# Differential attention of a hybrid layer: values stationary in column halves, heads in pairs, head norm in turned form

## What is computed

```python
lam = jnp.exp(jnp.sum(lp[0] * lp[1])) - jnp.exp(jnp.sum(lp[2] * lp[3])) + lam_init
...
logits = jnp.einsum('bqhrd,bshrd->bhrqs', qb, k).astype(jnp.float32) * (dq ** -0.5)
p = jax.nn.softmax(jnp.where(visible, logits, NEG_INF), axis=-1)
a = (p[:, :, 0] - lam * p[:, :, 1]).astype(v.dtype)
return jnp.einsum('bhqs,bshd->bqhd', a, v)
...
return head_rmsnorm(out, norm_g) * (1.0 - lam_init)
```

## Time and profile before

| | us |
|---|---|
| median of three runs (1865.95 to 1866.45) | 1865.99 |
| the profiled execution, whole | 1862.66 |
| its span | 1860.9 |
| TensorE, VectorE, ScalarE busy | 1735.6, 1454.9, 941.6 |
| D units, 397.4 to 670.3 | 272.9 |
| C and A pairs, 670.3 to 970.7 | 300.4 |

### The profile page before, as it was taken

How to read it: one execution, slowest core, us unless ns; L and a number is a source line. 1 busy time by engine, 2 the same in 40 slices (tenths; PEclk the granted TensorE clock), 3 DMA queues, 4 the chain that set the end, 5 groups by cost and what they waited for, 6 DMA issues and landing times. The chain is left out here.

```text
span 1860.9 us, 24050 instructions
## 1 busy us (share of the span) xinstructions
PE 1735.6 (93%) x8722; PEld 1313.2 (71%) x8722; DVE 1454.9 (78%) x2094; ACT 941.6 (51%) x1207; POOL 152.1 (8%) x129
## 2 busy tenths in 40 slices
PE   7999999999999999999999989759999999999980
PEld 7768877777777777777767767647777777777750
DVE  5587869989788878766529965669999999999966
ACT  6533121133334445545556610138877878777752
POOL 1100000000000000000000000012122122122103
PEclk9999999999999999999999999769999999999995
DMA  5202222112443322323216810379999999999937
GB/s 198 68 11 82 85 75 69 57 57 74 155 140 120 111 69 63 140 64 98 85 46 243 332 51 34 151 278 369 388 397 407 394 398 402 396 397 400 405 118 287
DMA packets 75920, 358.76 MB, mean 193 GB/s; under 512 B 8636, under 2 KB 11228, under 8 KB 49340
## 3 DMA queue, kind: packets, MB, share of 16 engines
q1 hardware_dynamic: 66364, 324.08, 46.8%
q0 software_dynamic: 5888, 20.97, 3.4%
q10 hardware_dynamic: 3584, 12.58, 1.7%
HBM read 301.63 MB, written 55.98 MB: 192 GB/s over the span
## 5 line engine op out<-in xcount | busy, mean ns | idle before, releaser
L2357 DVE TENSOR_TENSOR wa_lo<-wa,w_hi 128x2048 fp32r<-128x2048 f32 x127 | 287.5, 2286 | 14.9 <-ACT w_hi L2270 13.5
L2270 ACT ACTIVATE w_hi<-wa 128x2048 fp32r<-128x2048 f32 x127 | 242.8, 1915 | 63.0 <-PE psum L2215 36.4
L1470 PE MATMUL psum<-h_hi,w_hi 128*128 128x512 f32 x512 | 212.7, 415 | 4.2 <-DVE w_lo L153 2.1
L1470 PE MATMUL psum<-h_hi,w_lo 128*128 128x512 f32 x512 | 205.2, 401 | 0.0
L1470 PE MATMUL psum<-h_lo,w_hi 128*128 128x512 f32 x512 | 202.5, 395 | 0.0
L167 DVE MAX8 top<-sel 128x8 f32<-128x384 f32 (+5 forms) x192 | 171.4, 893 | 4.8
L2364 DVE TENSOR_TENSOR wb_lo<-wd,w_hi 128x2048 fp32r<-128x2048 f32 x64 | 143.8, 2289 | 33.9 <-ACT w_hi L2279 33.9
L165 DVE MATCH_REPLACE8 sel<-top,sel 128x384 f32<-128x384 f32 (+5 forms) x192 | 168.2, 876 | 0.0
L2199 PE MATMUL psum<-w_hi,xT_hi 128*96 128x512 f32 x512 | 164.5, 402 | 1.9 <-DVE xT_lo L2372 1.9
L2199 PE MATMUL psum<-w_hi,xT_lo 128*96 128x512 f32 x512 | 160.6, 394 | 0.0
L2199 PE MATMUL psum<-wa_lo,xT_hi 128*96 128x512 f32 x512 | 160.5, 395 | 0.0
(11 more groups left out here) (372 smaller groups left out, 3380.6 us busy)
## 6 DMA issues: line engine op xcount, KB each, us to landing
wa<-expert_up SPq DMA_DIRECT2D x128, 1024.0 KB, 10.4
wd<-expert_down SPq DMA_DIRECT2D x64, 1024.0 KB, 10.5
w<-w_gate SPq DMA_DIRECT2D x32, 512.0 KB, 4.2
gate_pre<-gate_out SPq DMA_DIRECT2D x64, 256.0 KB, 3.3
gate<-gate_pre SPq DMA_DIRECT2D x32, 512.0 KB, 5.7
ys<-yo ACTq DMA_DIRECT2D x32, 384.0 KB, 6.9
w<-w_T SPq DMA_DIRECT2D x18, 512.0 KB, 3.9
ys<-zeros SPq DMA_DIRECT2D x7, 1152.0 KB, 5.9
```

The lines of the kernel that those rows point to most:

```text
L1470: ins = nc.tensor.matmul(psum[:, 7, :], w[:, k, :], x[:, k, half * 512:(half + 1) * 512], start=(n == 0), stop=(n == BURST - 1))
L2270: nc.scalar.activation(hi_a(j, q).rearrange("p c m n -> p (c m n)"), wa[j][q][:, :, :, :].rearrange("p c m n -> p (c m n)"), ACT.Copy).the ...
L2357: nc.vector.tensor_tensor(wa_lo[j][q][:, :, :, :].rearrange("p c m n -> p (c m n)"), wa[j][q][:, :, :, :].rearrange("p c m n -> p (c m n)" ...
```

## The change

1. **Weights times values in D** as in C and A: values stationary, two heads together, after the turns of the second head; the first head of a pair has no `weigh`. All turns of a unit come at once. `weigh` is one function now.
2. **First map scaled by ScalarE.** `inverse` (VectorE) and `scale` (ScalarE) run for D too: `scale(u)` stands behind the second exponential and ahead of `gate_store`, `inverse(u)` behind `maxima(u)`. `differ` waits for `scaled`. `norm` only copies, one unit later for blocks 0 to 6.
3. **Head norm of D in turned form.** The output is already turned, so the 16 transposes go. Squares at NB + 2; then a string of 4 matmuls with a 128 x 128 matrix of two 64 x 64 blocks of ones, after unit NB + 8, sums them over each head's partitions (f32, 512 columns each); ScalarE takes the root of 512 columns each, four times; VectorE takes the reciprocal of the whole [128, 2048] in place at NB + 12 and multiplies at NB + 13. At NB + 3, NB + 8 and NB + 9 selections stand now.
4. B's string comes after unit 11 instead of 10. GpSimd sets the matrix of ones (3 memsets). The gain is loaded as [128, 2]. SyncE stores D at k = 41 from q2, behind `y_ready`.

```diff
-    s.gainB, s.gainD = sb("gainB", [P, W], 197.25), sb("gainD", [P, W], 198.25)
+    s.gainB, s.gainD = sb("gainB", [P, W], 197.25), sb("gainD", [P, 2], 198.25)
...
-    Y_AT = {"D": 10, "C": 16}
+    Y_AT = {"D": 11, "C": 8}
...
+                        if n == 0:
+                            sp.wait_ge(pt_copied, copied_by["B"])
+                        else:
+                            sp.wait_ge(y_ready, 2)
+                        sp.dma_start(s.yT_back[n], (s.k1, s.q2)[n][:, :, :]).then_inc(yT_stored, 16)
...
+            link(pool.memset(halves[:, :], 0.0))
+            link(pool.memset(halves[0:HD, 0:HD], 1.0))
+            pool.memset(halves[HD:P, HD:P], 1.0).then_inc(halves_ready, 1)
...
+                    if what == "D":
+                        act.wait_ge(aneg_ready, 1)
+                        nc.scalar.activation(sq[:, c, t0 * P:(t0 + 4) * P], src, ACT.Sqrt, bias=eps[:, 0:1],
+                                             scale=1.0 / HD).then_inc(pt_copied, 1)
...
                 if u < NB:
                     act.wait_ge(stats_ready, n_exp[u] + 2)
                     diff_exp(1)
+                    scale(u)
                 if u and u - 1 in burst_after:
                     gate_store(burst_after[u - 1])
...
-                link(nc.vector.reciprocal(inv[:, :], sums[:, b % 2, :, 0]))
-                nc.vector.tensor_tensor(token_heads(kind, b),
-                                        psum[:, 6, 0:W].rearrange("p (c h d) -> p c h d", c=2, d=HD),
-                                        by_head(inv[:, :]), ALU.mult).then_inc(out_normed, 1)
+                nc.vector.tensor_copy(out_of[kind][:, :, b * P:(b + 1) * P],
+                                      psum[:, 6, 0:2 * P].rearrange("p (c n) -> p c n", c=2)).then_inc(out_normed, 1)
...
-                link(nc.vector.scalar_tensor_tensor(out=stat[:, v % 4, 5:6], in0=stat[:, v % 4, 4:5],
-                                                    scalar=sums[:, b % 2, h, 0:1], in1=lam[:, 4:5],
-                                                    op0=ALU.mult, op1=ALU.mult))
+                link(nc.vector.tensor_tensor(stat[:, v % 4, 5:6], stat[:, v % 4, 4:5], lam[:, 4:5], ALU.mult))
+                dve.wait_ge(scaled, v + 1)
...
+                y, h = s.q2, u % NH
                 if u == NB + 2:
+                    nc.vector.tensor_tensor(sq[:, :, :], y[:, :, :], y[:, :, :], ALU.mult).then_inc(squared, 1)
+                elif u == NB + 12:
+                    dve.wait_ge(pt_copied, copied_by["D"])
+                    link(nc.vector.reciprocal(sq[:, :, :], sq[:, :, :]))
+                elif u == NB + 13:
+                    for c in range(2):
+                        ins = nc.vector.scalar_tensor_tensor(out=y[:, c, :], in0=y[:, c, :], scalar=gain_T[:, c:c + 1],
+                                                             in1=sq[:, c, :], op0=ALU.mult, op1=ALU.mult)
...
                 maxima(u)
+                inverse(u)
...
+                    if what == "D":
+                        pe.wait_ge(squared, 1)
+                        pe.wait_ge(halves_ready, 1)
+                        nc.tensor.matmul(psum[:, 4 + i % 2, :], halves[:, :], sq[:, c, t0 * P:(t0 + 4) * P],
+                                         start=True, stop=True).then_inc(pt_ready, 1)
...
+                for g in range(n):
+                    if i + g >= 2:
+                        pe.wait_ge(pt_copied, i + g - 1)
+                    turn(i + g)
+                for g in range(2):
+                    gate(gates_before(what) + (2 + g) * quarter, quarter)
+                    if h % 2 and g < n:
+                        m = weighed[0]
+                        weigh(i - n + g, i + g, m + g, m + n + g, 2 if n == 1 else 1 + 2 * g)
```

More of the change, by code:

```diff
@@ L991, in attend @@
     pt = [sb(f"pt{i}", [P, 512], 155.25 + 2 * i) for i in range(4)]
-    sq = sb("sq", [P, NT * NH, HD], 163.25)
+    sq = sb("sq", [P, 2, SEQ], 163.25)
+    halves = sb("halves", [P, P], 203.5)
     bias = sb("bias", [P, NH, BAND], 112.25)
@@ L1341, in inverse @@
                 _, b, h = units[u]
-                dve.wait_ge(exp_done, n_exp[u + 1])
+                dve.wait_ge(exp_done, n_exp[u] + 1)
                 nc.vector.reciprocal(stat[:, u % 4, 6:7], sums[:, b % 2, h, 0:1]).then_inc(inv_ready, 1)
             def more(u):
-                heads = q_of["D"][:, :, :].rearrange("p c (n d) -> p (c n) d", d=HD)
-                h = u % NH
+                y, h = s.q2, u % NH
                 if u == NB + 2:
[L1350 to L1362, removed]
+                    nc.vector.tensor_tensor(sq[:, :, :], y[:, :, :], y[:, :, :], ALU.mult).then_inc(squared, 1)
[6 more added lines that the diff above has]
+                                                             in1=sq[:, c, :], op0=ALU.mult, op1=ALU.mult)
+                    ins.then_inc(y_ready, 1)
                 else:
@@ L1430, in _, with weigh @@
             values = {"D": s.v2, "C": s.v1, "A": s.v2}
[L1432 to L1434 removed]
+            def weigh(i0, i1, m0, m1, freed):
+                u, g0, ng, last = groups[i0]
                 kind, b, h = units[u]
                 k0, nk = keys(kind, b)
[L1437 to L1458 removed]
+                pe.wait_ge(pt_copied, i1 + 1)
+                if h == 0 and g0 == 0 and u:
+                    pe.wait_ge(out_normed, u // NH)
+                for j in range(ng):
+                    for r, m in enumerate((m0, m1)):
+                        ins = nc.tensor.matmul(psum[HD * r:HD * r + HD, 6, h // 2 * P:(h // 2 + 1) * P],
+                                               values[kind][:, k0 + g0 + j, (h + r) * HD:(h + r + 1) * HD],
+                                               pt[m % 4][:, j * P:(j + 1) * P],
+                                               start=(g0 + j == 0), stop=(g0 + j == nk - 1))
+                ins.then_inc(pv_done, freed)
             def gate(first, count):
@@ L1482, in weigh_waiting @@
                     i = waiting.pop()
-                    weigh(i, weighed[0])
-                    weighed[0] += 1 if units[groups[i][0]][0] == "D" else 2
+                    weigh(i, i + 1, weighed[0], weighed[0] + 1, 2)
+                    weighed[0] += 2
             def turn(i):
@@ L1533, in _ @@
                     continue
-                if i >= 2:
-                    pe.wait_ge(pt_copied, i - 1)
-                quarter = BURST // 4
-                if g0 == 0:
-                    if what + 1 < NB:
-                        score(what + 1, 1)
-                    else:
-                        score(NB, 2)
-                    if what:
-                        gate(gates_before(what), 2 * quarter)
-                    pe.wait_ge(diff_ready, what + 1)
-                turn(i)
-                if last:
-                    gate(gates_before(what) + 2 * quarter, quarter)
-                weigh_waiting()
-                waiting.append(i)
-                if last:
-                    gate(gates_before(what) + 3 * quarter, quarter)
-                    weigh_waiting()
+                if g0:
+                    continue
+                quarter, n = BURST // 4, 1 if last else 2
+                if what + 1 < NB:
+                    score(what + 1, 1)
+                else:
+                    score(NB, 2)
+                if what:
+                    gate(gates_before(what), 2 * quarter)
+                pe.wait_ge(diff_ready, what + 1)
+                for g in range(n):
[7 more added lines that the diff above has]
+                        weigh(i - n + g, i + g, m + g, m + n + g, 2 if n == 1 else 1 + 2 * g)
+                if h % 2:
+                    weighed[0] += 2 * n
             weigh_waiting()
```

61 lines of the change are left out of this document (14 added, 47 removed).

## The result

| | us |
|---|---|
| median after (7 runs, 1871.8 to 1873.68) | 1873.10 |
| median before, run beside it (7 runs, the three shown before among them) | 1868.02 |
| ratio | 1.0032, interval 1.0023 to 1.0041 |
| profiled execution after, its span | 1873.68, 1871.9 |

The account below looks back on a forecast made before the run. TensorE, 93% busy, was taken as the bound. The terms -11.6 - 0.3 + 0.5 + 0.45 + 10.2 + 1.9 = +1.15 gave a median of 1867.1 us, no change that can be told; range 1861.5 to 1872.5 us.

Parts of the forecast that it names:

- Step 1: Weights times values in D with values stationary, two heads together: TensorE gains 11.6 us, from 31.0 to 19.4.
- The number of switches is the same 80: TensorE in D: switches between gates, weighing and scores stay at 80, so the change adds no switching cost.
- the upper of the two values given: Gain of weighing in D: 11.6 us taken, or 12.5 if 0.1 more ahead of scores in some last groups is counted.
- holds both: TensorE in D: C's 1.03 us for eight products already includes parallel tiles and the loss at each switch of mode.
- Step 2: First map of D scaled by ScalarE ahead of the gate store: costs nothing, with a cover that thins.
- 0.7 to 1 us: ScalarE's gate store in D's narrower blocks: slack left before TensorE needs bank 7, with the scaling ahead of it.
- Step 3: B's string, one unit later in D: +0.5 us, with the granted clock falling behind it again.
- it falls again, at the same price: Behind B's string the granted clock falls to 0.50 as before, at an unchanged cost.
- Step 4: D's string of four float32 products and roots: 2.85 us instead of 2.42, +0.45.
- Step 5: VectorE's 2048-column reciprocal in C: 12.1 us, stalling TensorE once by 10.2 us, plus 1.9 for the clock.
- rival B: VectorE at NB + 12: reciprocal of 14.7 us or more; at 17 us, stall 15.1 and time 1872.0 us; chance 0.12.
- The 0.3 that the border was to give back: Border from D to C: the changes around scaling and norm give back about 0.3 us, summed as -0.3.

Follow-up runs that it names:

- the second traces: The kernel before and the changed kernel, each run once more with no edit: 1866.2 us (ratio 0.9999) and 1872.93 us (ratio 1.0034).

## Why the prediction was wrong

**Step 1, where it failed.** `weigh` was worth 12.5 us (31.8 to 19.3), the upper of the two values given. The failed sentence is "The number of switches is the same 80", by which the gates around `weigh` cost nothing more. Leaving the turns aside, the traces have 128 changes of work in D before and 104 after; of these, changes of the tile's shape are 64 before and 104 after. The old `weigh` had the shape of the gates, and only the scores had another. Now the 24 groups of `weigh` have a third shape, 16 of them in the middle of the gates and 8 ahead of the scores, and in the 24 other places the gates end at the scores, where a `weigh` of their own shape stood between. Between the second traces the gates of the 32 units grow by 4.3 us (184.4 to 188.7), and the 48 ends of 0.09 us alone come to that. The prediction had set 0.9 us against such ends, which is why it took 11.6 and not 12.5; the term was too small by 3.4. The waits for the store ahead of the gates in units 2 to 7 add 1.0. D gained 7.5 instead of 11.1. The rule was on the table: the Trainium skill's TensorEngine Tiling (Array Packing), section on the key properties, says that a change of mode drains the array, and I set it aside because C's 1.03 us "holds both". It doesn't: the cost lies outside those 1.03 us, in the neighbours. The place is shown by the run with the weighing behind the gates, which takes back some 5 us by moving it alone; that the shape is what costs there is read from the gaps, 0.23 against 0.32.

**Step 2.** The scaling cost nothing, as forecast, to 0.02 us a unit. But in the narrow blocks the store's slack of "0.7 to 1 us" was below nothing with no scaling at all, since the `weigh` that covered it had gone. That belongs to step 1: I named the cover for the widest block only.

**Step 3.** +0.5 was +0.2 between traces with the clock up (turns and transposes 0.3 less, the time ahead of the gates behind the string 0.5 more). The dip behind the string isn't in every trace of the kernel before, so "it falls again, at the same price" was a guess from one trace; the range had room for it.

**Step 4.** 3.86 us (703.30 to 707.16) instead of 2.85, against 2.42 before: +1.44 for +0.45. The price of a product was wrong. 0.43 us came from scores of 32 rows; a float32 product of 512 columns with all 128 rows takes two records of 0.43, 0.86 us at the full clock, so the four take 3.4 back to back. The waits for roots that the prediction added hardly occur: the third product waited some 0.1 us for the first root, and after that ScalarE, whose roots take 0.69 us and not 0.60, waited for the products (start us, us; in brackets the idle time):

```profile
703.30 3.94 PE L1509 MATMUL psum<-sq,halves 128*128 128x512 f32 x8
706.41 0.69 ACT L1201 ACTIVATE sq<-psum,eps 128x512 f32<-128x512 f32 x1 [0.41 <-PE psum L1509]
```

The second table load, which the prediction put into the stall, costs its 0.6 us one pair earlier, in a wait for `gate_out`.

**Step 5, right in the main.** 12.95 us for 12.1 (6.3 ns a column, so rival B's eight full passes did not come), one stall in the pair named, half clock behind it. The gates behind the scores of NB + 16 began 9.9 us later than without the reciprocal. The sum had 10.2 + 1.9 = 12.1, the runs 11.1, of which 0.64 is a small trail that the prediction excluded (TensorE waits once more, 0.58 us, for VectorE's copy at L1290). The wait began one step earlier than written, at the banks of the scores.

**Together.** Inside `attend` the second traces differ by +6.2 us where the sum had +1.15: D 3.6 worse than summed, C 1.5: the string with its table load 1.6 and the border 0.7 worse, the stall and clock 1.0 better. The 0.3 that the border was to give back were 0.4 more instead, since the last pair's `weigh` and gates fall there, and with the weighing behind the gates it gave back 0.4. The direction of each large part was right; with 12 us won and 12 lost, the small terms decided the sign.

## What to carry to other kernels

A new tile shape on TensorE costs at its edges, in the rows of its neighbours: count changes of shape, and put work of one shape together at a place where the shape changes anyway. One long instruction on an engine that others wait for costs its whole length; cut into pieces no longer than what they replace, it costs nothing (12.95 us in one piece 11.1, in eight light pieces, 1.75 us each in place of 2.5 us of selections, none that shows). And when work is taken from between two users of a buffer, ask what it was hiding.

## What the runs showed of the hardware

The last of a run of gates takes 0.23 us up to work of shape 128*128 and 0.32 up to work of shape 128*64 or 32*128, in all the edges of D. A dip of the granted clock to 0.50, worth 1.5 us, came in some traces of a kernel and not in others (behind B's string in the kernel before, at the border to C in the changed one), while the one at the wait of 7.9 us came in both traces. A reciprocal on VectorE costs 6.3 ns a column at 2048 columns, 6.8 at 256. A float32 product of 512 columns and 128 rows costs TensorE 0.86 us. GpSimd's power costs 160 ns a column and stops part of VectorE's operations meanwhile.
